# Starting places in a partition: the gated block of an expert layer on multiples of 2048 bytes

## The reference

```python
def peer_ffn(x, w_q, sub_keys, u_tab, v_tab):
    q = (x @ w_q).reshape(n, PEER_HEADS, 2, PEER_HALF)
    s = einsum('thpd,phkd->thpk', q, sub_keys)      # top 16 of each half, top 16 of their sums: idx, top_s
    ...
    g = softmax(top_s)
    act = gelu(einsum('thkd,td->thk', u_tab[idx], x))
    return einsum('thk,thkd->td', g * act, v_tab[idx])
```

## The kernel before

| tensor | start | past a multiple of 64 | past a multiple of 256 | past a multiple of 2048 |
|---|---|---|---|---|
| `xh` (row c at + 2080 c, second half at + 1040) | 44928 | 0 | 128 | 1920 |
| `uh`, `ul` (buffer + 4096, chunk + 512) | 69824, 86208 | 0 | 192 | 192 |
| `xl` | 134240 | 32 | 96 | 1120 |
| `onej`, `onei` | 167072, 175264 | 32 | 160 | 1184 |
| `gated` | 167072 | 32 | 160 | 1184 |
| `sact` | 169120 | 32 | 160 | 1184 |
| `ah` (two buffers of 2048) | 170144 | 32 | 160 | 160 |
| `al` (two buffers of 2048) | 174240 | 32 | 160 | 160 |
| slabs of the query projection, gates `g` | 183520 | 32 | 224 | 1248 |
| mix_in, mix_out, pw1: slabs, input high, low | 107328, 123712, 140352 | 0 | 64, 64, 64 | 832, 832, 1088 |
| pw2: slabs, input high, low | 123968, 140352, 156992 | 0 | 64, 64, 64 | 1088, 1088, 1344 |

## Time and profile before

### The profile page before, as it was taken

How to read it: one execution, slowest core, us unless ns; L and a number is a source line. 1 busy time by engine, 2 the same in 40 slices (tenths; PEclk the granted TensorE clock), 3 DMA queues, 4 the chain that set the end, 5 groups by cost and what they waited for, 6 DMA issues and landing times. The chain is left out here.

```text
span 4425.3 us, 74431 instructions
## 1 busy us (share of the span) xinstructions
PE 4168.4 (94%) x27209; PEld 3713.9 (84%) x27209; DVE 2531.1 (57%) x4688; ACT 1180.9 (27%) x1587; POOL 39.1 (1%) x43
## 2 busy tenths in 40 slices
PE   8778679999999999999998987999999999999997
PEld 8754479999999998888887567999999998888886
DVE  3642246777776435555554746787777525555554
ACT  2101142233333321111113443223333321111112
POOL 0000000000000010000000000000000001000000
PEclk9868789999999999999999999999999999999999
DMA  3026523335444565555541012334454466555552
GB/s 110 20 87 199 179 81 103 113 130 182 148 167 164 190 227 194 180 195 177 198 139 67 28 38 96 107 123 141 167 181 157 166 210 212 190 183 194 179 195 79
DMA packets 321924, 652.36 MB, mean 147 GB/s; under 512 B 26241, under 2 KB 157442, under 8 KB 321154
## 3 DMA queue, kind: packets, MB, share of 16 engines
q1 hardware_dynamic: 318978, 642.36, 43.1%
q0 software_dynamic: 2816, 8.40, 0.5%
HBM read 509.00 MB, written 141.53 MB: 147 GB/s over the span
## 5 line engine op out<-in xcount | busy, mean ns | idle before, releaser
L1796 DVE TENSOR_TENSOR experts_ul<-experts_u,experts_uh 128x1024 fp32r<-128x1024 f32 x512 | 627.0, 1225 | 1113.5 <-ACT experts_uh L1690 1106.1
L1583 PE MATMUL ps<-peer_x_then_r_xh,experts_ul 128*128 128x260 f32 x4096 | 1168.0, 285 | 0.0
L1584 PE MATMUL ps<-experts_over_x_xl,experts_uh 128*128 128x260 f32 x4096 | 1158.1, 283 | 0.0
L1585 PE MATMUL ps<-peer_x_then_r_xh,experts_uh 128*128 128x260 f32 x4096 | 1155.3, 282 | 0.0
L1690 ACT ACTIVATE experts_uh<-experts_u 128x1024 fp32r<-128x1024 f32 x512 | 540.3, 1056 | 1134.4 <-PE ps L1647 1125.0
L1647 PE MATMUL ps<-experts_over_a_ah,experts_uh 128*128 128x512 f32 x2048 | 810.0, 396 | 0.0
L1645 PE MATMUL ps<-experts_over_a_ah,experts_ul 128*128 128x512 f32 x2048 | 810.0, 395 | 0.0
L1646 PE MATMUL ps<-experts_over_a_al,experts_uh 128*128 128x512 f32 x2048 | 810.0, 395 | 0.0
L1583 PEld LDWEIGHTS ps<-peer_x_then_r_xh,experts_ul 128*128 128x128 f32 x4096 | 770.9, 188 | 0.0
L1585 PEld LDWEIGHTS ps<-peer_x_then_r_xh,experts_uh 128*128 128x128 f32 x4096 | 770.7, 188 | 0.0
L1584 PEld LDWEIGHTS ps<-experts_over_x_xl,experts_uh 128*128 128x128 f32 x4096 | 770.5, 188 | 0.0
(11 more groups left out here) (347 smaller groups left out, 4678.4 us busy)
## 6 DMA issues: line engine op xcount, KB each, us to landing
experts_u<-peer_u SPq DMA_DIRECT2D x256, 512.0 KB, 3.3
experts_u<-peer_v SPq DMA_DIRECT2D x256, 512.0 KB, 3.4
hidden<-experts_act SPq DMA_DIRECT2D x256, 260.0 KB, 2.1
gates<-experts_over_b_g SPq DMA_DIRECT2D x128, 512.0 KB, 3.1
experts_over_b_g<-gates SPq DMA_DIRECT2D x128, 512.0 KB, 5.0
experts_act<-hidden SPq DMA_DIRECT2D x256, 256.0 KB, 3.6
mla_ct<-cache SPq DMA_DIRECT2D x64, 320.0 KB, 3.7
pa_ct<-cache SPq DMA_DIRECT2D x64, 320.0 KB, 3.8
```

Source lines behind the costliest of these rows:

```text
L1583: pe.matmul(o, ul[:, b % 4, c], xh[:, c, t], start=(c == 0), stop=False)
L1584: pe.matmul(o, uh[:, b % 4, c], xl[:, c, t], start=False, stop=False)
L1585: mm = pe.matmul(o, uh[:, b % 4, c], xh[:, c, t], start=False, stop=(c == KC - 1))
L1796: v.tensor_tensor(ul[:, b % 4], u[:, b % 2], uh[:, b % 4].bitcast(F32), ALU.subtract).then_inc(split_done, 1)
```

## The change

The start of every overlay is rounded up to a multiple of 64 bytes and no longer of 32. In the second set of `over_a`, the next start after `gated` is rounded up to a multiple of 2048, `ah` and `al` are placed there, and `sact` follows them.

```diff
@@ class Overlay @@
         self.nc, self.name = nc, f"{s.name}_{name}"
-        self.at = (nc.sbuf_base + 31) // 32 * 32
+        self.at = (nc.sbuf_base + 63) // 64 * 64
         self.end = self.at + size
         s.sb(name, [P, size // 4 + 16])
@@ def peer_experts @@
         then = over.row()
         gated = then.sb("gated", [P, TP])
-        sact = then.sb("sact", [P, TS, P // 4])
+        then.at = (then.at + 2047) // 2048 * 2048
         ah = then.sb("ah", [P, 2, TP], F32R)
         al = then.sb("al", [P, 2, TP], F32R)
+        sact = then.sb("sact", [P, TS, P // 4])
```

## The result

The changed kernel takes 4400.51 us (median of 4 runs, 4392.84 to 4403.33) against 4424.81 for the kernel before; the ratio is 0.9941, with a 95% interval of 0.9923 to 0.9958. That is 24 us less where 40 were forecast. The profiled execution took 4403.33 us with a span of 4401.5, so 23.8 us of span are to be explained.

A forecast was written before the change was run, and what follows sets the result against it. TensorE was taken as the bound, the output stage being its matmuls times the distance between starts. Gated parts -39 and other overlays -1 gave -40 us: 4385 us against the 4424.91 median, range 4308 to 4434.

The forecast's parts named there:

- The bound: Output stage (applies the second expert table): time is 6144 matmuls times 233.3 ns between starts, 1433 us; TensorE never waits.
- The count near 3080: Sign that the forecast is right: matmuls in a 700 us window of the output stage rise from 3001 to near 3080.
- The term of the gated parts: Output stage: new starts of ah and al speed each 512-column matmul by 6.3 ns, -39 us over 6144 matmuls.
- The triples of c = 1 and c = 4: Hidden stage, three 260-column matmuls per c: 0.37 us at c = 1, 0.35 at c = 4; their difference would give 81 us.
- nothing left over: Output stage: ah and al started 160 past a multiple of 2048, 32 past one of 64; afterwards no remainder, no half crosses.
- The other overlays: Hidden stage: rounding to 64 moves xl, over_a and over_b by 32 bytes; -8 to +5 us, taken as -1.
- All of it goes: Rival, output stage: the pace reaches 215 ns a matmul, -112 us, giving 4313 us; 22%.
- Places do not matter: Rival, TensorE: lateness is a rate at which f32r columns are read, whatever the starts; 4425 us within 8.8; 24%.
- A worse pace: Rival, output stage: weight and moving reads both begin on multiples of 64 and hold each other up; 4442 us; 14%.

The follow-up runs named there:

- the run with ah and al apart: Changed kernel with ah and al in 4096-byte slots, given different starts every 16 blocks, weights at 192: 5.440 to 5.627 us a block of 24 matmuls.
- The sweep: Changed kernel with ah and al in 4096-byte slots, their common start moved every 16 blocks of the output stage: 5.440 to 5.653 us a block.
- the last run: Changed kernel with ah and al starts moved every 16 blocks, output-stage operands taken as plain f32: 20.600 us a block at all 16 places, kernel 8270 us.
- the sweep of the weights: Changed kernel with ah and al starts moved every 16 blocks, weights uh and ul at 0 (layer 0) or 64 (layer 1): 5.440 to 5.622 us a block.
- both single-half runs: Changed kernel with overlays still rounded to 32, only ah, al, sact moved: 4399.06 us; kernel before with only overlays rounded to 64: 4388.12 us.
- The run with the hidden places: Changed kernel with each half row of xh and xl in 1280 bytes, all starting alike: hidden stage 950.8 us in layer 0, 961.5 in layer 1.

## Why the prediction was right, and where it was not

**The bound.** That the output stage is the number of its matmuls times the distance between two starts, and that nothing hides behind it or becomes the bound, was right: both traces have full windows up to the end of the stage and no wait of TensorE there. The count near 3080 that was named as a sign was met by luck: 3074 holds matmuls of the next work, and the pace alone gives 3058.

**The term of the gated parts.** The mechanism, a pace that hangs on the start of the moving operand, was right, and its size was too large: -39 us forecast, -27.3 measured. The step that was off is the scaling of 3.2 ns a matmul of 260 columns to 6.3 for 512. Measured are 4.4. Scaling by matmul gave 3.2, scaling by columns 6.3, and the truth is between. The triples of c = 1 and c = 4 were closer to the case than I knew: their xh has the distances 224 and 64, the very ones that ah has before and after. But each holds a matmul on xl at some third distance, and the run with ah and al apart shows that such steps cost by themselves. So their difference (81 us) was three times too large, and the difference to the mean, which I took, 1.4 times. The sweep is the comparison that was missing.

**The reason given for it.** I put the gain to "nothing left over" against 64 or 2048. This was wrong: places 64 and 128 past a multiple of 2048 are as slow as 160, and 192 is faster than 0. What counts is the start against the weights' start, modulo 256.

**The other overlays.** -1 forecast, within -8 to +5. Measured are +1.4 us for the hidden stages. It didn't come from where the forecast put it: the blocks of 48 matmuls alone kept their 5.753 us with xl in its new place, and all of it lies in the blocks that also hold gate matmuls. There the one-hot matrices moved by 32 bytes as well as xl, and no run moves one without the other.

**The rivals.** *All of it goes*: no place came near 215 ns; the best is 226.7. The 215 itself was half of a row of plain f32, and the last run shows that such a row is one of two for a product. A matmul of 512 f32r columns in 215 ns has been seen in no run here. The Trainium skill (TensorE: Matmul & The Clock Gate, Back-to-back issue gap) has N/2.4 + 2.5 ns for an isolated warm matmul; no run here shows it for f32r, the nearest being 226.7 against its 215.7. *Places do not matter* falls with the sweeps; its best argument, the same pace of pw1 and pw2, holds because the shift of 256 bytes leaves every distance as it is. By the rule of the Trainium skill's SBUF page (SBUF — State Buffer, Door 1) on 16-byte lines, 0 and 160 would have been equal: here they differ by 0.107 us a block. The Trainium skill (TensorE: Matmul & The Clock Gate, Step-by-step) also says that loading the next weights does not take read bandwidth from the running matmul; the sweep of the weights shows the pace of a moving operand that stays where it is changing by up to 0.16 us a block with the weights' place, though no run shows that bandwidth is the cause. *A worse pace* had its mechanism upside down: reads that begin at like places are the fastest, not the slowest.

**What is shown and what is argued.** Shown is that the pace of f32r matmuls of 512 columns depends on the difference of two starts modulo 256, from 226.7 to 235.5 ns, and that plain f32 at half the rate doesn't depend on it. For 260 columns the stage times and most blocks follow the same order, but a second pace at identical places appears too. That the two reads meet in some part of the memory that repeats every 256 bytes is the simplest reading, and no run shows it. Nor is it known why a mixture of starts costs what it does.

## What to carry to other kernels

When TensorE is busy all the time, divide a stretch of the time line by its matmuls: a constant pace above the best one seen is not waiting, and it can hang on where the operands start. Place f32r moving operands and weights so that all starts leave the same remainder modulo 256, and choose row strides that keep it (here 1280 bytes for 1040 of data); that is free but for some bytes. An alignment that helps should be swept before it is explained, since a round number can be right for another reason: 2048 gave two thirds of the gain here, and 64 unused bytes ahead of the weights gave the rest.

## What the runs showed that was not expected

The paces are few and exact: 5.440, 5.493, 5.547, 5.600, 5.653 us a block, 0.053 apart (2.2 ns a matmul), each held to the ns over 15 blocks; distance 160 and the splits are the exceptions. And 260-column stages can run at either of two paces at the same places: the 48 matmuls of mix_in and pw1 took 5.73 or 5.77 us in the traces of different kernels, mix_in 5.77 in the profiles of before and after but 5.73 in both single-half runs. It is worth about 1 us in each such stage. The run with the hidden places shows the same within one execution, with all starts alike: 5.70 in some stretches and 5.76 in others. It was not studied.
